# A hybrid decoder layer in split fp32: the first four weight units computed side by side, plain tiles over all eight PSUM banks, VectorE's list reordered

## The reference

```
h = h + 0.5 * swiglu(rmsnorm(h, ffn1_norm), ffn1_w_gate, ffn1_w_up, ffn1_w_down)
u = rmsnorm(h, mix_norm)
proj = u @ w_in                     # pooling input, q, k, v, two gates
merged = gate_pool * branch_pool + gate_attn * branch_attn
h = h + merged @ w_out
h = h + 0.5 * swiglu(rmsnorm(h, ffn2_norm), ffn2_w_gate, ffn2_w_up, ffn2_w_down)

def swiglu(x, w_gate, w_up, w_down):
    return (silu(x @ w_gate) * (x @ w_up)) @ w_down
```

## Time and profile before

| | us |
|---|---|
| median of 3 runs (lowest to highest) | 1081.14 (1077.69 to 1082.23) |
| the profiled execution | 1081.94 |
| its span | 1080.1 |
| TensorE busy | 1051.6 |
| VectorE busy | 656.3 |
| ScalarE busy | 478.0 |
| GpSimd busy | 434.1 |

### The profile page before, as it was taken

How to read it: one execution, slowest core, us unless ns; L and a number is a source line. 1 busy time by engine, 2 the same in 40 slices (tenths; PEclk the granted TensorE clock), 3 DMA queues, 4 the chain that set the end, 5 groups by cost and what they waited for, 6 DMA issues and landing times.

```text
span 1080.1 us, 15526 instructions
## 1 busy us (share of the span) xinstructions
PE 1051.6 (97%) x6024; PEld 914.7 (85%) x6024; DVE 656.3 (61%) x1008; ACT 478.0 (44%) x825; POOL 434.1 (40%) x240
## 2 busy tenths in 40 slices
PE   6889999999999999999999999999999999999998
PEld 5769999998888777887777788888889999998887
DVE  5899767758440276425676756668986667685101
ACT  6334555556331233335777653343344554553110
POOL 1433342335434435344454535444323423344441
PEclk9999999999999999999999999999999999999999
DMA  7434776733332422222111113216257757433232
GB/s 277 116 97 115 189 196 158 188 106 98 98 98 97 137 88 98 78 78 80 58 58 58 59 59 98 98 39 199 95 119 187 198 163 187 117 104 98 98 98 98
DMA packets 42033, 126.35 MB, mean 117 GB/s; under 512 B 4336, under 2 KB 4336, under 8 KB 41968
## 3 DMA queue, kind: packets, MB, share of 16 engines
q1 hardware_dynamic: 37216, 108.41, 30.3%
q0 software_dynamic: 4608, 16.78, 9.1%
q10 hardware_dynamic: 144, 0.26, 0.1%
HBM read 123.34 MB, written 2.10 MB: 116 GB/s over the span
## 4 chain that ended last, share of the span: by engine, by line
PE 80%; DVE 12%; ACT 3%; DMA 2%; issue 2%; SPq 0%; DVEq 0%; ACTq 0%
PE psum L478 16%; PE psum L480 15%; PE psum L479 15%; PE psum L531 10%; PE psum L532 9%; PE psum L533 9%; PE psum L755 1%; DVE gate L1389 1%; DVE moving_sums_low L1424 1%; PE psum L770 1%; DVE hidden L1393 1%; DMA w_raw<-weights_dram 1%; PE psum L783 1%; DVE u_blocks_low L1419 1%; PE psum L784 1%
## 5 line engine op out<-in xcount | busy, mean ns | idle before, releaser
L1246 POOL TENSOR_TENSOR w_low_in_place<-w_raw,w_high 128x1024 fp32r<-128x1024 f32 x66 | 163.4, 2480 | 209.9 <-ACT w_high L850 209.8
L850 ACT ACTIVATE w_high<-w_raw 128x1024 fp32r<-128x1024 f32 x116 | 122.2, 1055 | 210.6 <-DMA w_raw<-weights_dram 169.0
L1246 POOL TENSOR_TENSOR w_low<-w_raw,w_high 128x1024 fp32r<-128x1024 f32 x50 | 122.7, 2456 | 118.5 <-ACT w_high L850 118.5
L478 PE MATMUL psum<-hidden_high,w_high 128*128 128x512 f32 x352 | 137.0, 389 | 0.0
L479 PE MATMUL psum<-hidden_low,w_high 128*128 128x512 f32 x352 | 137.0, 389 | 0.0
L480 PE MATMUL psum<-hidden_high,w_low_in_place 128*128 128x512 f32 x352 | 136.9, 389 | 0.0
L1356 DVE SCALAR_TENSOR_TENSOR h<-psum,h 128x512 f32<-128x512 f32 x24 | 16.5, 689 | 150.9 <-PE psum L480 150.9
L478 PE MATMUL psum<-u_high,w_high 128*128 128x512 f32 x240 | 99.8, 416 | 0.5 <-DVE u_low L1345 0.5
L479 PE MATMUL psum<-u_low,w_high 128*128 128x512 f32 x240 | 94.4, 394 | 0.0
L480 PE MATMUL psum<-u_high,w_low 128*128 128x512 f32 x240 | 94.4, 394 | 0.0
L478 PE MATMUL psum<-ffn_u_high,w_high 128*128 128x512 f32 x192 | 78.7, 410 | 15.4 <-DVE gate L1378 7.1
(11 more groups left out here) (251 smaller groups left out, 2910.1 us busy)
## 6 DMA issues: line engine op xcount, KB each, us to landing
w_raw<-weights_dram SPq DMA_DIRECT2D x117, 512.0 KB, 3.5
gate_a<-weights_dram SPq DMA_DIRECT2D x16, 512.0 KB, 6.3
gate_s<-weights_dram SPq DMA_DIRECT2D x16, 512.0 KB, 3.6
gate_s<-weights_dram POOLq DMA_DIRECT2D x16, 512.0 KB, 6.4
up_a<-weights_dram SPq DMA_DIRECT2D x16, 512.0 KB, 4.8
up_s<-weights_dram SPq DMA_DIRECT2D x16, 512.0 KB, 3.6
up_s<-weights_dram POOLq DMA_DIRECT2D x16, 512.0 KB, 8.6
gate_a<-weights_dram SPq DMA_DIRECT2D x16, 256.0 KB, 5.3
```

The source lines that it names most:

```text
L478: pe.matmul(o, wh, xh, start=start, stop=False)
L850: act.activation(high[:, s, :], raw[:, s, :], ACT.Copy).then_inc(high_done, 1)
L1246: pool.tensor_tensor(wlow[:, s, :], raw[:, s, :], high[:, s, :], ALU.subtract).then_inc(low_done, 1)
```

## The change

Four things are changed.

1. The first FFN's units 0 to 3. The first halves of their columns (tiles 0 to 3) are loaded in four quarters: a quarter is two tiles of two units, 256 KB. The order of the quarters is units 0 and 1, units 2 and 3, then the same for the next two tiles; the second halves follow, one unit each. TensorE computes the first tile of units 0 and 1 together, product by product, then the quarters in that order, four banks side by side, and then the second half of each unit. The ones product moves from the middle of unit 2 to before unit 3's second half, and GpSimd makes two of the low halves. The squares get three more buffers. The gate weights of the first pairs are loaded after unit 6 and no longer after unit 4.
2. Banks. Tile f uses banks `plain_bank(f)` and the next: 4, 6, 0, 2, 4, 6, so tiles 2 and 3 wait for no bank (bank 3 for the variance), and the ones product of both FFNs goes into bank 3. Waits of the first pair and of ScalarE's first copy are relaxed to match.
3. VectorE's list in `plain`, for both FFNs: up's `weight_sums` and `low_a1` come before the gate's s2 and s31 and before tile 5's scaling, with a wait for unit 10; NT2 and NT1 come later, and T3, B22 and T4 come last.
4. ScalarE's list in `plain`: in both FFNs tile 4's tanh and up's a1 copy come before the gate's s2 and s31 copies; in the first, units 5 to 7 are refilled before the first tanh, unit 8 before the block copies, unit 9 before the copies of the moving sums, unit 10 behind them, and unit 11 behind tile 2's tanh.

The diff, cut to its core:

```diff
+QUARTERS = ((0, 0), (2, 0), (0, 1), (2, 1))
...
+SUM_BANK = (3, 0, 3)
+def plain_bank(f):
+    return 2 * ((f + 2) % 4)
...
+            def load_quarter(i):
+                u, cols = QUARTERS[i][0], slice(QUARTERS[i][1] * 2 * P, (QUARTERS[i][1] + 1) * 2 * P)
+                sp.dma_start(raw[:, u:u + 2, cols], weights_in[u:u + 2, :, cols].rearrange("u p n -> p u n")
+                             ).then_inc(quarter_landed[i], 16)
+            def load_second_half(u):
+                sp.dma_start(raw[:, u, UNIT // 2:UNIT], weights_in[u, :, UNIT // 2:UNIT]).then_inc(raw_landed[u], 16)
...
             load_x(0)
-            sp.dma_start(raw[:, 0, 0:UNIT // 2], weights_in[0, :, 0:UNIT // 2]).then_inc(first_landed, 16)
+            load_quarter(0)
             load_x(1)
-            sp.dma_start(raw[:, 0, UNIT // 2:UNIT], weights_in[0, :, UNIT // 2:UNIT]).then_inc(raw_landed[0], 16)
-            for i in range(2, len(X_PIECES) - 1):
-                load_x(i)
-            load(1)
-            load(2)
+            load_quarter(1)
+            load_x(2)
+            load_quarter(2)
+            load_quarter(3)
+            load_x(3)
+            load_second_half(0)
+            load_x(4)
+            for u in range(1, SLOTS):
+                load_second_half(u)
             sp.dma_start(consts[:, :], consts_in).then_inc(consts_landed, 16)
-            load(3)
-            load_used(4)
-            gate_prologue(0)
-            for u in range(5, U_DN1):
+            for u in range(SLOTS, U_DN1):
                 load_used(u)
+                if u == SLOTS + 2:
+                    gate_prologue(0)
...
+            def first_tile(xh, xl):
+                first = range(2)
+                def product(w, x, start):
+                    for s in first:
+                        pe.matmul(psum[:, 4 + s, :], w[:, s, 0:P], x[:, 0, :], start=start, stop=False)
+                pe.wait_ge(u_high[0], 1)
+                pe.wait_ge(quarter_high, 1)
+                product(high, xh, True)
+                pe.wait_ge(u_low[0], 1)
+                product(high, xl, False)
+                pe.wait_ge(quarter_low, 1)
+                product(raw_low, xh, False)
+            def first_units(xh, xl):
+                first_tile(xh, xl)
+                for i, (u, part) in enumerate(QUARTERS):
+                    pe.wait_ge(quarter_low, i + 1)
+                    for c in range(2 * part, 2 * part + 2):
+                        pe.wait_ge(u_low[0], c + 1)
+                        for s in (u, u + 1):
+                            if i or c:
+                                passes(4 + s, s, c, xh[:, c, :], xl[:, c, :], c == 0, False, raw_low)
+                for s in range(SLOTS):
+                    if s == SLOTS - 1:
+                        sum_of_squares(0)
+                    if s < 2:
+                        pe.wait_ge(quarter_low, len(QUARTERS) + 1 + s)
+                    else:
+                        pe.wait_ge(low_done, lows(s))
+                    for c in range(TILES // 2, TILES):
+                        pe.wait_ge(u_low[0], c + 1)
+                        mm = passes(4 + s, s, c, xh[:, c, :], xl[:, c, :], False, c == TILES - 1, raw_low)
+                    mm.then_inc(unit_used, 1)
...
                 for f in range(2, PLAIN[n]):
                     k = f % 2
-                    pe.wait_ge(F["gate_scaled"], f - 1)
-                    project(base + 2 * f, 2 * k, 4 + 2 * k, xh, xl, wlow=raw_low)
-                    pe.wait_ge(F["up_scaled"], f - 1)
-                    project(base + 2 * f + 1, 2 * k + 1, 5 + 2 * k, xh, xl, wlow=raw_low)
+                    if f >= 4:
+                        pe.wait_ge(F["gate_scaled"], f - 3)
+                    project(base + 2 * f, 2 * k, plain_bank(f), xh, xl, wlow=raw_low)
+                    if f >= 4:
+                        pe.wait_ge(F["up_scaled"], f - 3)
+                    elif plain_bank(f) + 1 == SUM_BANK[2 * n]:
+                        pe.wait_ge(var_ready, 2 * n + 1)
+                    project(base + 2 * f + 1, 2 * k + 1, plain_bank(f) + 1, xh, xl, wlow=raw_low)
...
-                        pe.wait_ge(F["up_scaled" if k else "gate_scaled"], PLAIN[n] - 1)
+                        pe.wait_ge(F["up_scaled" if k else "gate_scaled"], PLAIN[n] - 3)
...
+                    else:
+                        pe.wait_ge(F["up_scaled" if k else "gate_scaled"], PLAIN[n] - 2)
...
                 g = first_pair(n)
-                next_unit(base)
-                next_unit(base + 1)
+                if n:
+                    next_unit(base)
+                    next_unit(base + 1)
+                else:
+                    next_unit(base + 1)
+                    next_unit(base + 2)
+                    next_unit(base + 3)
                 gate_tanh_tile(0, F)
-                next_unit(base + 2)
+                next_unit(base + (2 if n else 4))
                 for b in (B11, B21, B22):
                     block_high(n, b)
-                next_unit(base + 3)
+                if n:
+                    next_unit(base + 3)
                 gate_tanh_tile(1, F)
-                next_unit(base + 4)
+                next_unit(base + (4 if n else 5))
                 for t, count in ((NT2, 2), (NT1, 2), (T3, 3), (T4, 4)):
                     sum_high(n, t, count)
-                next_unit(base + 5)
+                next_unit(base + (5 if n else 6))
                 gate_tanh_tile(2, F)
-                next_unit(base + 6)
+                next_unit(base + (6 if n else 7))
                 high_a1(g, gate_w)
-                next_unit(base + 7)
+                if n:
+                    next_unit(base + 7)
                 gate_tanh_tile(3, F)
+                gate_tanh_tile(4, F)
+                high_a1(g, up_w)
                 high_s2(g, gate_w)
                 high_s31(g, gate_w)
-                gate_tanh_tile(4, F)
-                high_a1(g, up_w)
                 gate_tanh_tile(5, F)
                 high_s2(g, up_w)
                 high_s31(g, up_w)
...
-                    act.wait_ge(F["hidden"], PLAIN[n])
+                    act.wait_ge(F["hidden"], PLAIN[n] - 1)
...
             scale_high(0, 0)
-            act.wait_ge(first_landed, 16)
-            act.activation(high[:, 0, 0:UNIT // 2], raw[:, 0, 0:UNIT // 2], ACT.Copy).then_inc(first_high, 1)
+            quarter(0)
             scale_high(0, 1)
-            act.wait_ge(raw_landed[0], 16)
-            act.activation(high[:, 0, UNIT // 2:UNIT], raw[:, 0, UNIT // 2:UNIT], ACT.Copy).then_inc(high_done, 1)
-            for c in range(2, DT):
-                scale_high(0, c)
-            act.wait_ge(raw_landed[1], 16)
-            act.activation(high[:, 1, 0:UNIT // 2], raw[:, 1, 0:UNIT // 2], ACT.Copy).then_inc(first_high, 1)
-            act.activation(high[:, 1, UNIT // 2:UNIT], raw[:, 1, UNIT // 2:UNIT], ACT.Copy).then_inc(high_done, 1)
+            quarter(1)
+            scale_high(0, 2)
+            scale_high(0, 3)
+            quarter(2)
+            quarter(3)
+            scale_high(0, 4)
+            scale_high(0, 5)
+            second_half(0)
+            scale_high(0, 6)
+            scale_high(0, 7)
+            for u in range(1, SLOTS):
+                second_half(u)
             for c in range(DT):
                 square(0, c, c)
-                if c == 3:
-                    refill(2, 2, 1, first=True)
-            refill(3, 3, 1, first=True)
+            next_unit(U_GU1)
...
                 plain_hidden(2, F)
                 block_low(n, B11, 1)
                 block_low(n, B21, 2)
-                sum_low(n, NT2, 4)
-                sum_low(n, NT1, 5)
                 plain_scaled(base, 3, F)
                 plain_hidden(3, F)
                 weight_sums(g, gate_w)
                 low_a1(g, gate_w)
+                plain_scaled(base, 4, F)
+                plain_hidden(4, F)
+                dve.wait_ge(unit_used, base + 2 * PLAIN[n] - 1)
+                weight_sums(g, up_w)
+                low_a1(g, up_w)
+                sum_low(n, NT2, 4)
+                low_s2(g, gate_w)
+                sum_low(n, NT1, 5)
+                low_s31(g, gate_w)
+                plain_scaled(base, 5, F)
+                low_s2(g, up_w)
+                plain_hidden(5, F)
+                low_s31(g, up_w)
                 sum_low(n, T3, 6)
                 block_low(n, B22, 3)
                 sum_low(n, T4, 7)
-                plain_scaled(base, 4, F)
-                plain_hidden(4, F)
-                low_s2(g, gate_w)
-                low_s31(g, gate_w)
-                plain_scaled(base, 5, F)
-                weight_sums(g, up_w)
-                low_a1(g, up_w)
-                plain_hidden(5, F)
-                low_s2(g, up_w)
-                low_s31(g, up_w)
```

More of the change, by code:

```diff
@@ L480, in passes, with project @@
                 return pe.matmul(o, wl, xh, start=False, stop=stop)
[L482 to L484 removed]
+            def project(u, s, bank, xh, xl, x_ready=None, tiles=range(TILES), wlow=low):
```

(12 more changed lines are left out.)

87 lines of the change are left out of this document (55 added, 32 removed).

## The result

| | before | changed |
|---|---|---|
| median of 7 runs | 1080.26 us (1077.24 to 1082.72) | 1085.2 us (1084.3 to 1086.37) |
| ratio to before, 95% interval | | 1.0047 (1.0031 to 1.0063) |
| profiled execution | 1081.94 (span 1080.1) | 1085.03 (span 1083.2) |

A forecast was written before the change was run, and what follows sets the result against it. TensorE, 97% busy, could win only waits and slow clock, so the change of S in each half plus clock counted: -4.0 + 2.5 = -1.5 on 1081.94 gives 1080.4, expected median 1079.6 us, range 1071.5 to 1084.5.

The forecast's parts named there:

- The start: First half, units 0 to 3: first matmul near 6.0, unit 3 ending at 30.7 against 34.8, 4.1 us sooner.
- VectorE's norm factor: First half: long list starts at 28.1, 1.5 us later; factor done at 40.5, first gate and up scaled at 41.7.
- The new wait at unit 10: First half: TensorE waits 3.0 us for unit 10's low part, ready at 66.4, and loses 1.7 by the clock.
- Up's low and S, first half: Up's low ends at 83.0, but ScalarE's copy behind tanh 5 holds S to 90.3; 4.0 us gained after clock loss.
- S: Moment when TensorE starts the gate's s2 product; before, at 95.97 in the first half and 801.00 in the second.
- After S: Pair 0, first half: list ends about 99.6, before the a22 product at 103.5; nothing later depends on the plain stage except through S.
- Second half, S: Up's sums wait 5.5 us for the accumulating transfer; S at 801.8 against 801.00, with 1.7 of clock: 2.5 us lost.
- The clock: Shortly after a TensorE wait the granted clock falls to 0.50 for 3.4 us, losing 1.7 us of work.
- S follows up's low: Both halves: ScalarE's copy stays hidden, S at 85.9 and 797.4, gains of 10.1 and 3.6: 1067.4 us; chance 0.11.
- TensorE alone: TensorE alone is the bound; all four of its waits and their clock loss go: 1061.4 us; chance 0.05.
- Nothing shifts: S unchanged in both halves, the four waits turning into others: 1081 us; chance 0.07.
- Slower: Accumulating transfer heads VectorE's list, uncovered in the second half; 7 us later landing in each half gives 1088; chance 0.07.

The follow-up runs named there:

- adds first: Changed kernel with pair 0's add of the gate's s3 part ahead of pair 1's weight sums in both halves: 1080.64 us, ratio 0.9991 to the kernel before.
- the start alone: Changed kernel with VectorE's and ScalarE's plain-stage lists back in the old order, new start and banks kept: 1083.07 us, ratio 1.0016 to the kernel before.
- the order alone: Kernel before with only the new order of VectorE's and ScalarE's lists and the copy's wait belonging to it: 1088.43 us, ratio 1.0067.
- the filled idle time: Changed kernel; in the second half VectorE does seven items ahead of the wait for unit 10 and up's accumulated weights: 1079.53 us, ratio 0.9993 to before.
- new order in the first half only: Changed kernel with pair 0's s3 add ahead of pair 1's weight sums and, in the second half, VectorE's and ScalarE's old lists: 1078.26 us, ratio 0.9982.
- copy first: Changed kernel with ScalarE's copy of the gate's first partial product moved before unit 5's tanh and up's high sums: 1089.49 us, ratio 1.0089 to before.
- two small moves of adds and lows: Changed kernel with pair 0's s3 add moved ahead in both halves and VectorE's seven items ahead of its second-half wait: 1074.83 us, ratio 0.9956 to before.

## Why the prediction was wrong, step by step

- **The start**: right. The first matmul at 6.30 (forecast 6.0), the variance at 28.09 (28.1), no stop between. 4 us ahead of before.
- **VectorE's norm factor**: right in sum, wrong in its parts, so the sum is luck. The first gate is scaled at 37.7, not 41, since unit 7's load came late (ScalarE's copy waited 6.50 us for it) and GpSimd was idle; the low parts then met the eight scaled blocks, 11.18 us for the forecast 7.5, and the list was level with the forecast again behind them (50.0 for 49.2).
- **The new wait at unit 10**: right. 3.66 us on a low part at 67.11, forecast 3.0 at 66.4; clock behind it 0.50.
- **Up's low and S, first half**: right. 83.36 and 90.42, forecast 83.0 and 90.3, the wait put on ScalarE's copy behind tanh 5 (ScalarE's rows: tanh at 87.95, the copy at 89.95, 0.36 long).
- **After S**: here it failed. The prediction held that the rest of the list "ends about 99.6, before the a22 product at 103.5; pair 1's first low is there at 102.9 for 106.4", and that nothing later depends on the plain stage but through S. The list did end at 100.0 and the product was due at 103.6. But between the two stand two adds and 5.9 us of pair 1's weight work, and the add for a22 behind them: 106.98. The end of the plain stage's list was held against the product; the product waits for the tenth item behind that end. The cost: 3.44 us in the first half, 2.65 and 1.7 of clock in the second. The run with the adds first shows it: both waits go. The trace of before had the warning, an add that ended at 106.50 for a product at 107.49; with the ten items behind the list written out, the wait would have stood in the sum.
- **Second half, S**: the wait for the accumulating transfer came (6.38 us, forecast 5.5), and S lay 0.8 us nearer to its landmark, not 0.8 further, since the transfer was issued sooner (782.68, 7.1 us ahead of the landmark, before 6.2) and VectorE could go on 5.5 us behind the issue, not 6.2. 1.7 of clock was right. The step is mis-sized by 1.6 us, to the other side of the failure.
- **The clock**: the prediction has it fall "a few tenths of a microsecond" behind a wait. In its own rows it fell at 39.40, 1.2 us after TensorE went on at 38.24; the 1.7 us of each stretch, which its sum used, were right at S in both halves. Two of its additions are off by 0.2 and 0.1 us (28.1 + 0.7 + 0.7 + 3.4 is 32.9, not 33.1; the four steps to ScalarE's copy are 2.5, not 2.6), which changes nothing.
- **The sum**: first half -4.0 forecast, 0.0 measured; second +2.5 forecast, +5.2 measured; 2.0 won between them that the sum didn't have (1.1 at pair 1 and some 0.8 around 384 us, by the same landmarks in SP's timeline and the clock, 0.96 before and 1.00 after from 380 to 420 us). The second part goes with the clock and not with the edit, see below.
- **The rivals**: "S follows up's low" and "TensorE alone" had the wrong idea of what bounds. "Nothing shifts" had the first half's number for another reason. "Slower" named the accumulation, which was not late: the loss came from a mechanism that no case had. Even so the shape of the error is one that the rivals should have held: the last consumer of the same list.

What spreads the executions of one kernel over some 6 us (1077.75 to 1083.71 of the kernel before) the traces show in part. TensorE has the same work in all 13 kernels from the end of the first half's pairs (SyncE's first `w_raw` issue behind them, near 238 us) to unit 11 of the second half. It took 550.9 to 551.0 us in the five traces in which the clock fell once, from 380 to 400 us; 552.4 in the two in which it fell once, from 420 to 440; 552.8 to 553.4 in the four with both; and 554.0 in the two in which it was low for twice as long from 420 to 440. The changed kernel is of the second kind, the kernel before and the adds first of the third. Differences of up to 3 us between two executions can come from there, whatever the edit. Pairs 1 to 7 before it took 126.8 to 128.9 us; what spreads these isn't shown.

Open: what makes the clock fall there in one execution and not in the next; why the start alone and the order alone were each 2 to 3 us slower than expected; and whether the 2 us by which the adds first and the filled idle time fell short in the median are lost in the pairs behind pair 0, as the traces with the adds first suggest, or lie within the uncertainty. A version free of the S wait without a longer list was not tried.

## What to carry to other kernels

When a queue's list is the bound, moving an item ahead of a wait moves every item behind it back: follow each item up to the end of the next stage, and ask of each product which item it waits for, not when the list ends. A gain at the front of a bound list shows only when the last wait of that list has gone too: here start and order together cost 5 us, and with two small moves of adds and lows on top they gave 0.4% on the kernel before. Look first at how much each such item had to spare before the change: the add for a22 had 0.99 us. A wait put down to "issue" has no releaser in the profile; all four of these were semaphore waits, which the code names.

## What the runs showed of the hardware

- Moving GpSimd's operations off VectorE's lows moved the hold-up, almost unchanged in sum (4.2 us less, then 3.7 more), onto VectorE's next operations with two SBUF inputs: 1.22 for 2.31 us there, 1.35 to 2.13 for 0.67 to 1.23 here. VectorE's adds that read PSUM took 0.41 or 0.42 in both.
- What the clock takes behind a wait doesn't follow from the wait's length. A wait of 3.44 us before a22 had no low clock behind it (changed kernel), one of 3.46 at the same product 1.7 us lost (idle time filled). Waits of 1.94 (kernel before, 796.52) and 2.71 (new order in the first half only) had 1.7 behind them, one of 1.33 (start alone) none. Of two waits of 4.55 (copy first) one had a low stretch of 3.4 us behind it, at 816.42, the other one of twice that length around it.
